# The recurrence's score products of a stick-breaking / HGRN2 / MoE layer, in blocks of 32 tokens instead of 64

## What is computed

```python
b = jnp.cumsum(fb, axis=2)
diff = b[:, :, :, None, :] - b[:, :, None, :, :]
decay = jnp.where(causal, jnp.exp(jnp.where(causal, diff, 0.0)), 0.0)
scores = jnp.einsum('bhtc,bhsc,bhtsc->bhts', qb, kb, decay)
o = jnp.einsum('bhts,bhsv->bhtv', scores, vb) + jnp.einsum('bhtc,bhcv->bhtv', qb * jnp.exp(b), s)
s_new = jnp.exp(b_last[:, :, 0, :])[..., None] * s + jnp.einsum('bhsc,bhsv->bhcv', kb * jnp.exp(b_last - b), vb)
```

## Time and profile before

| | |
|---|---|
| median of 3 runs | 2429.89 us (2425.22 to 2437.62) |
| the profiled execution: its time, its span | 2428.82 us, 2426.9 us |
| TensorE busy | 2284.9 us, 94% of the span |
| VectorE, ScalarE, GpSimd busy | 1405.8, 963.1, 1496.5 us |
| mean granted clock of TensorE | 0.987 of full |

### The profile page before, as it was taken

How to read it: one execution, slowest core, us unless ns; L and a number is a source line. 1 busy time by engine, 2 the same in 40 slices (tenths; PEclk the granted TensorE clock), 3 DMA queues, 4 the chain that set the end, 5 groups by cost and what they waited for, 6 DMA issues and landing times. The chain is left out here.

```text
span 2426.9 us, 40519 instructions
## 1 busy us (share of the span) xinstructions
PE 2284.9 (94%) x15460; PEld 2011.2 (83%) x15460; DVE 1405.8 (58%) x2749; ACT 963.1 (40%) x1582; POOL 1496.5 (62%) x1525
## 2 busy tenths in 40 slices
PE   4999999999999999999998999999999999999882
PEld 4889899898898998989987776578898888888882
DVE  7365665755756647557567697534455555555344
ACT  3452734526436346263364232122323333333334
POOL 6355674675646646657467256577667777776533
PEclk9999999999999999999998999999999999999996
DMA  5201112011011111111112641599999999999995
GB/s 181 77 28 45 41 45 60 29 44 50 29 45 49 46 50 37 36 50 37 47 38 78 194 133 47 154 281 300 310 348 350 354 352 350 351 352 360 363 353 181
DMA packets 210602, 380.72 MB, mean 157 GB/s; under 512 B 25810, under 2 KB 132558, under 8 KB 209898
## 3 DMA queue, kind: packets, MB, share of 16 engines
q1 hardware_dynamic: 180218, 302.25, 34.8%
q0 software_dynamic: 30192, 75.89, 13.1%
HBM read 310.71 MB, written 76.41 MB: 160 GB/s over the span
## 5 line engine op out<-in xcount | busy, mean ns | idle before, releaser
L128 PE MATMUL ps<-xTh,w_mix_low 128*128 128x368 f32 (+1 forms) x1728 | 594.1, 344 | 7.0 <-POOL w_mix_low L122 5.7
L130 PE MATMUL ps<-xTh,w_mix_high 128*128 128x368 f32 (+3 forms) x1808 | 598.9, 331 | 0.4 <-issue 0.4
L129 PE MATMUL ps<-xTl,w_mix_high 128*128 128x368 f32 (+3 forms) x1808 | 597.1, 330 | 1.5 <-issue 1.5
L2298 POOL DMA_INDIRECT xg_early<-h_d,tabq_early x304 | 313.2, 1030 | 153.8 <-issue 80.8
L129 PEld LDWEIGHTS ps<-xTl,w_mix_high 128*128 128x128 f32 (+1 forms) x1808 | 340.1, 188 | 15.8 <-issue 9.5
L128 PEld LDWEIGHTS ps<-xTh,w_mix_low 128*128 128x128 f32 x1728 | 329.3, 191 | 20.5 <-issue 15.4
L130 PEld LDWEIGHTS ps<-xTh,w_mix_high 128*128 128x128 f32 (+1 forms) x1808 | 339.4, 188 | 5.6 <-issue 1.8
L2310 POOL DMA_INDIRECT ys_d<-yo,tab_early x114 | 216.6, 1900 | 112.6 <-issue 50.6
L122 POOL TENSOR_TENSOR w_mix_low<-w_mix_raw,w_mix_high 128x1024 fp32r<-128x1024 f32 x72 | 182.7, 2537 | 120.9 <-ACT w_mix_high L117 83.1
L1333 POOL TENSOR_TENSOR x_m<-x_m,kh_m 128x128 f32<-128x128 f32 (+1 forms) x272 | 125.4, 461 | 114.6 <-ACT x_m L866 114.6
L2340 PEld LDWEIGHTS ps<-xgT,wg_early 128*128 128x128 f32 x1376 | 177.6, 190 | 19.3 <-issue 18.6
(11 more groups left out here) (396 smaller groups left out, 4558.8 us busy)
## 6 DMA issues: line engine op xcount, KB each, us to landing
wd_early<-in_w_exp_down SPq DMA_DIRECT2D x43, 1024.0 KB
wg_early<-in_w_exp_gate SPq DMA_DIRECT2D x82, 512.0 KB
wu_early<-in_w_exp_up SPq DMA_DIRECT2D x82, 512.0 KB
w_mix_raw<-in_w_in SPq DMA_DIRECT2D x72, 512.0 KB, 3.8
wg<-in_w_exp_gate SPq DMA_DIRECT2D x42, 512.0 KB
wu<-in_w_exp_up SPq DMA_DIRECT2D x42, 512.0 KB
wd<-in_w_exp_down SPq DMA_DIRECT2D x21, 1024.0 KB
xg_early<-h_d,tabq_early POOLq DMA_INDIRECT x316
```

The costliest lines, as they stand in the source:

```text
L128: pe.matmul(out, ll, rh, start=start, stop=False)
L129: pe.matmul(out, lh, rl, start=False, stop=False)
L130: return pe.matmul(out, lh, rh, start=False, stop=stop)
L2298: pool.indirect_dma_start(out=xg[:, b, g, :], out_offset=None, in_=h2_d[:, :].rearrange("t (q n) -> (t q) n", q=4), in_offset=bass.Indirec ...
```

## The change

The block becomes 32 tokens, so there are six planes (the diagonal and the levels 1 to 16), and each has up to four products of 32 by 32, which go to four groups of 32 partitions. The level of 32 leaves the masked planes and becomes, like the level of 64, a product between the two halves without a mask (one for each 64 tokens). VectorE masks the six planes (192 columns), copies the level of 32 (two copies of 32x32) and of 64 (one of 64x64) from PSUM into aT, sums the planes of all 128 partitions in one reduce into a compact tile `diagonal`, waits for it, and copies its four blocks into their place in aT. All of aT is cleared once, since more blocks of it stay zero. One mask level less is built at the entry, and the masks are cut out in four copies instead of two. The second meaning of the name LATE is renamed BEHIND, so that the routing reads the constant 65536 again and not 6; no instruction is added or removed by that.

```diff
@@ -56,8 +56,9 @@
 SLOTS = NE * CAP + OVB * P
 LEVELS = [1, 2, 4, 8, 16, 32, 64]
 NL = len(LEVELS)
-BLOCK = 64
+BLOCK, HALF = 32, 64
 PLANES = 1 + sum(2 * hw <= BLOCK for hw in LEVELS)
+ACROSS, HALVES = PLANES * BLOCK, (PLANES + 1) * BLOCK
 CHUNKS = [(0, 368), (368, 368), (736, 352)]
 (C_SQ, C_SK, C_SV, C_HQ, C_HF, C_HI, C_HG, C_GS, C_GH) = range(0, 9 * D, D)
 
...
@@ -368,24 +369,25 @@
+        diagonal = sb("diagonal_m", [P, 2, BLOCK])
-            CONSTANTS = 3 + 3 * (PLANES - 1) + 2 + 2
+            CONSTANTS = 3 + 3 * (PLANES - 1) + 2 + P // BLOCK
...
@@ -676,10 +678,13 @@
                         for i in range(PLANES - 1):
                             for b in range(0, m, BLOCK):
                                 xs = x[:, slot, i, xo + b:xo + b + BLOCK]
-                                mm = pe.matmul(ps[b:b + BLOCK, bank, (i + 1) * BLOCK:(i + 2) * BLOCK], xs, xs, start=True, stop=True)
+                                pe.matmul(ps[b:b + BLOCK, bank, (i + 1) * BLOCK:(i + 2) * BLOCK], xs, xs, start=True, stop=True)
+                        for b in range(0, m, HALF):
+                            mm = pe.matmul(ps[b:b + BLOCK, bank, ACROSS:ACROSS + BLOCK], x[:, slot, NL - 2, xo + b:xo + b + BLOCK],
+                                           x[:, slot, NL - 2, xo + b + BLOCK:xo + b + HALF], start=True, stop=True)
                         if m == P:
-                            mm = pe.matmul(ps[0:BLOCK, bank, PLANES * BLOCK:(PLANES + 1) * BLOCK], x[:, slot, NL - 1, xo:xo + BLOCK],
-                                           x[:, slot, NL - 1, xo + BLOCK:xo + P], start=True, stop=True)
+                            mm = pe.matmul(ps[0:HALF, bank, HALVES:HALVES + HALF], x[:, slot, NL - 1, xo:xo + HALF],
+                                           x[:, slot, NL - 1, xo + HALF:xo + P], start=True, stop=True)
                         mm.then_inc(p_done, 1)
                         if j:
                             pe.wait_ge(ke_copied, j)
...
@@ -1135,14 +1140,17 @@
                             dve.wait_ge(a_done, j - 1)
                             dve.wait_ge(y_done, j - 1)
                         planes = ps[:m, PB[j % 2], 0:PLANES * BLOCK].rearrange("p (l t) -> p l t", l=PLANES)
-                        mm = dve.tensor_tensor(pm[:m, j % 2, :, :], planes, masks[:m, :, :], ALU.mult)
+                        dve.tensor_tensor(pm[:m, j % 2, :, :], planes, masks[:m, :, :], ALU.mult)
+                        for b in range(0, m, HALF):
+                            mm = dve.tensor_copy(aT[b:b + BLOCK, j % 2, b + BLOCK:b + HALF], ps[b:b + BLOCK, PB[j % 2], ACROSS:ACROSS + BLOCK])
                         if m == P:
-                            mm = dve.tensor_copy(aT[0:BLOCK, j % 2, BLOCK:P], ps[0:BLOCK, PB[j % 2], PLANES * BLOCK:(PLANES + 1) * BLOCK])
+                            mm = dve.tensor_copy(aT[0:HALF, j % 2, HALF:P], ps[0:HALF, PB[j % 2], HALVES:HALVES + HALF])
                         mm.then_inc(masked, 1)
                         dve.wait_ge(masked, j + 1)
+                        dve.tensor_reduce(diagonal[:m, j % 2, :], pm[:m, j % 2, :, :].rearrange("p l t -> p t l"), AX.X, ALU.add).then_inc(summed, 1)
+                        dve.wait_ge(summed, j + 1)
                         for b in range(0, m, BLOCK):
-                            mm = dve.tensor_reduce(aT[b:b + BLOCK, j % 2, b:b + BLOCK],
-                                                   pm[b:b + BLOCK, j % 2, :, :].rearrange("p l t -> p t l"), AX.X, ALU.add)
+                            mm = dve.tensor_copy(aT[b:b + BLOCK, j % 2, b:b + BLOCK], diagonal[b:b + BLOCK, j % 2, :])
                         mm.then_inc(a_done, 1)
 
                     def state(cn):
...
@@ -1219,7 +1227,7 @@
                 ch = Chain(dve, entry_s)
                 dve.memset(tri[:, :, :], 1.0).then_inc(memo, 1)
                 dve.memset(whole[:, :, :], 1.0).then_inc(memo, 1)
-                dve.memset(aT[BLOCK:P, :, 0:BLOCK], 0.0)
+                dve.memset(aT[:, :, :], 0.0)
                 dve.memset(small[:, 0:1], RMS_EPS).then_inc(memo, 1)
                 for t in range(NT):
                     statistics(t)
...
@@ -1256,7 +1264,7 @@
                     attention(h)
                     hgrn(h)
                 last_merge()
-                for k in range(EARLY, LATE):
+                for k in range(EARLY, BEHIND):
                     dve.wait_ge(wo_high, k + 1)
                     split_low(dve, wol[:, k, :], staged[k], woh[:, k, :]).then_inc(wo_rest, 1)
                 dve.wait_ge(row_high, 2)
```

More of the change, by code:

```diff
@@ L244, in __exit__ @@
         self.stack.close()
-FIRST, LATE = 5, 6
+FIRST, BEHIND = 5, 6
 COLUMNS = {"q": C_SQ, "k": C_SK, "v": C_SV, "hq": C_HQ, "hf": C_HF, "hi": C_HI, "hg": C_HG, "gs": C_GS, "gh": C_GH}
@@ L375, in mixer @@
                        "z_done abs_done e_done l_done z_copied sp_done hi_done lo_done c_done arg_done w_done o_done "
-                       "osb_copied pa pd diff_done exp_done eb_done qe_exp qe_done x_done p_done masked a_done ke_done ke_copied "
+                       "osb_copied pa pd diff_done exp_done eb_done qe_exp qe_done x_done p_done masked summed a_done ke_done ke_copied "
                        "y_done oT_copied su_done s_done sg_done silu_done g_done squares root_ready u_raw merged wo_in wo_high wo_low last_s par_in xr0 xr1 xr2 xr3 var_ready rstd_ready entry_s shift_ready normed scaled xn_ready turned x_high x_low xs0 xs1 xs2 xs3 "
@@ L380, in mixer @@
                 z_done, abs_done, e_done, l_done, z_copied, sp_done, hi_done, lo_done, c_done, arg_done, w_done, o_done,
-                osb_copied, pa, pd, diff_done, exp_done, eb_done, qe_exp, qe_done, x_done, p_done, masked, a_done, ke_done, ke_copied,
+                osb_copied, pa, pd, diff_done, exp_done, eb_done, qe_exp, qe_done, x_done, p_done, masked, summed, a_done, ke_done, ke_copied,
                 y_done, oT_copied, su_done, s_done, sg_done, silu_done, g_done, squares, root_ready, u_raw, merged, wo_in, wo_high, wo_low, last_s,
@@ L1407, in _ @@
                     hgrn(h)
-    return staged[LATE:]
+    return staged[BEHIND:]
 SHARED_SEMAPHORES = "kept yo0 yo1 yo2 yo3 xi0 xi1 stored0 stored1 y_left y_right x_clear tab_s early_in"
@@ L1512, in _ @@
             m_load(3)
-            sp.wait_ge(wo_low, HEADS - LATE)
+            sp.wait_ge(wo_low, HEADS - BEHIND)
             for dst, n in ((wg, "w_sh_gate"), (wu, "w_sh_up"), (wd, "w_sh_down")):
@@ L1553, in first_tile @@
                 for k in range(FIRST, HEADS):
-                    if k >= LATE:
-                        pe.wait_ge(wo_low, k - LATE + 1)
+                    if k >= BEHIND:
+                        pe.wait_ge(wo_low, k - BEHIND + 1)
                     for b in range(2):
@@ L1910, in tables @@
                     dve.tensor_copy(tabw[:, some, j], ps[:, RB, n * NE:(n + 1) * NE][:, some]).then_inc(tab_s, 1)
-            for k in range(LATE, HEADS):
-                split_low(dve, wol[:, k, :], late[k - LATE], woh[:, k, :]).then_inc(wo_low, 1)
+            for k in range(BEHIND, HEADS):
+                split_low(dve, wol[:, k, :], late[k - BEHIND], woh[:, k, :]).then_inc(wo_low, 1)
             dve.wait_ge(first_high, 1)
```

## The result

The changed kernel is slower, by half a percent. Its median is 2443.63 us (11 runs) against 2432.5 us of the kernel before beside it, ratio 1.005, 95% interval 1.0032 to 1.0067. I had forecast 2412.5 us with a range of 2402 to 2434, and slower had 13%, for a reason that did not come true.

What follows compares the result with a forecast made beforehand. TensorE's issue was taken to bound seven heads, the chain between engines the eighth. Savings of 13.3 us (seven heads) and 4 us (last head), 17.3 in all, from the 2429.89 us median gave 2412.5 us, range 2402 to 2434.

Steps and rivals of the forecast that it cites:

- TensorE's products: TensorE's products of one full chunk in the recurrence, first product to transpose: 0.83 us against 1.08, 0.25 less.
- that rival: Each TensorE record has a floor price (29 ns) however many column groups, making the kernel slower, 2464 us; chance 13%.
- The change of width from 32 to 64: TensorE going from 32-wide to 64-wide products in a full chunk: between nothing and 0.10 us, taken as 0.10.
- What of it arrives: TensorE's saving in heads 0 to 6: chunks 0 and 1 nothing, later ones all, 1.9 us a head, 13.3 in seven.
- the wait for the low weights: TensorE's wait for POOL's weights' low part between chunks 1 and 2: 0.83 us before, 1.3 after, in seven heads.
- the prediction's steps: TensorE's times read from the old trace: 0.17 us for L674, 0.70 for L679's 24 records, 0.10 back to full width.
- The four copies: VectorE's 32x32 copies within SBUF into aT: 0.06 to 0.18 us each, taken as 0.12, 0.48 in all per chunk.
- In heads 0 to 6 all this is covered and worth nothing: VectorE's saving of 0.97 us per chunk lies hidden behind TensorE in the first seven heads, so changes no time there.
- The last head: Eighth head's recurrence, bound by the chain between engines: 4 us less, bounds 1 and 6.
- The unit: VectorE's work on one full chunk's scores, from mask to next instruction: 1.78 us against 2.75, 0.97 less.
- the four units of my sum: VectorE's four score units before the fourth part's differences in the last head: 0.97 us saved each, 3.9 in all.
- the rest: Time from the output projection's first product, behind the barrier, to the end; taken as the same in both kernels.

Runs made afterwards that it cites:

- the direct sums: Changed kernel, but four 32x192 reduces write each block's sum straight into aT, replacing one reduce, its wait and four SBUF copies; 2425.78 us, ratio to before 0.9958.

## Why the prediction was wrong

**TensorE's products: right.** 0.86 us against 0.83, ten steps in 0.33 against 0.32, and four groups at no price per record: 40 records in 0.33 us are 8 ns each. Two side figures of that rival don't follow from its own sum, which gives 2451 us at 25 ns a record, not 2453, and has the kernel slower from some 17 ns on, not 15; nothing else rests on them. The change of width from 32 to 64, which no row of before showed, costs: without it the chunk takes 0.17 us less, though this saving has the shorter steps of the level of 64 in it.

**What of it arrives: too much.** I let chunks 2 to 7 and the chunk of 64 arrive, 1.9 us a head. With the copies out of the way it is 158.9 - 158.0 = 0.9 us. Chunks 0 and 1 are held by POOL as I said (the wait for the low weights 1.2 us, forecast 1.3). But chunks 7 and 8 are held as well, by ACT's chain before its copies of the keys. ACT in the kernel before, the chain's first row and the copy at its end:

```profile
240.02 0.48 ACT L787 ACTIVATE kT_m<-ps 128x368 f32<-128x368 f32 x1 [3.73 <-PE ps L130]
...
247.24 0.28 ACT L879 ACTIVATE ke_m<-ps 128x128 f32<-128x128 f32 x1
```

The chain begins behind a product of TensorE just ahead of chunk 7 (240.57), so the gain of chunk 6 still arrives, and what follows does not: from the start of chunk 6 to the last transpose it is 12.99 us before and 12.79 with the direct sums. The 0.98 us of the chunk of 64 were nearly all work (0.17 + 0.70 + 0.10 by the prediction's steps), but ACT's copy of the keys ended only 0.05 us before its transpose in the trace of before, and a shorter chunk just waits for it. What is left is chunks 2 to 6, some 0.2 us each.

**The four copies: the step that failed.** "The four copies in SBUF are in no row; between 0.06 and 0.18 start to start". Alone they take 0.18. Beside POOL they stand, 0.64 in the mean and up to 8.9 us. I looked for the price of the instruction and not for what it needs. The page of the Trainium skill that I cited gave the speed of such a copy; the Trainium skill also has the rule for the ports that it takes (cited above), which I didn't weigh. And the trace of before had the pattern, in a row of my own: the last line of the earlier trace rows is one difference with two sources in SBUF that took 2.29 us, where the thirteen behind it took 0.28 each. It ended 0.16 us behind this one, the last of POOL's products:

```profile
1300.90 0.71 POOL L1335 TENSOR_TENSOR x_m<-x_m,kh_m 128x256 f32<-128x256 f32 x1
```

The same happens the other way round. POOL's second product of a head, 0.5 us elsewhere, and VectorE's fifteen differences with two sources in SBUF beside it:

```profile
168.54 0.67 POOL L1333 TENSOR_TENSOR x_m<-x_m,kh_m 128x128 f32<-128x128 f32 x1 [2.63 <-ACT x_m L866]
169.17 3.65 POOL L1333 TENSOR_TENSOR x_m<-x_m,hq_m 128x128 f32<-128x128 f32 x1
```
```profile
169.19 2.90 DVE L1125 TENSOR_TENSOR x_m<-bT_m 128x128 f32<-128x128 f32 x14
172.02 0.41 DVE L1128 TENSOR_TENSOR x_m<-bT_m 128x256 f32<-128x256 f32 x1
```

VectorE's fifteen end at 172.43 and POOL's instruction at 172.82: the engines exclude each other, and in both places over a whole queue.

**"In heads 0 to 6 all this is covered and worth nothing": wrong.** VectorE's 9 us in chunk 0 are covered where they stand, but they move POOL's split, and TensorE pays 0.5 us for it at chunk 3. In the chunk of 64 both copies meet POOL's two long products and vrow is next in VectorE's queue: 1.4 us more. Measured, the copies cost 159.8 - 158.0 = 1.8 us a head, 12.6 in seven, and 3.1 more through the clock.

**The last head: the wrong sign.** Forecast 4 us less; it takes 4.8 more with the copies in SBUF, and 0.9 less with the sums in PSUM. The unit takes 2.2 us when nothing stands, forecast 1.78: the small copies out of PSUM cost 0.19 and not 0.13 each, and those in SBUF 0.18 and not 0.12. So a unit saves 0.55 us and not 0.97, some 2 us in the four units of my sum; why only 0.9 of them arrive no run shows.

Summed by the profiled executions: entry 2.6, seven heads 9.5 (6.4 of the copies net of the gain, 3.1 of the clock), last head 4.8, the rest 3.6 less, 13.4 in all (rounded), as the spans have it. The entry and the rest differ about as much between executions of kernels that do not differ there; that they nearly cancel is luck.

## What to carry to other kernels

Before an instruction is added to VectorE, look not only for its duration but at what POOL does at that time: a copy, a scaling or an operation with two sources, all in SBUF, can stand for POOL's work, while the same with a source in PSUM does not. A result that is only passed on is then better kept in PSUM. A stall that is covered where it stands can still come out elsewhere: the 8.9 us of chunk 0 became 0.5 us of TensorE at chunk 3. A saving on TensorE arrives only in those chunks that nothing else ends; where another engine ends just ahead of TensorE, as ACT did by 0.05 us in the chunk of 64, there is nothing to gain, though the trace shows no wait.

## What I had not expected of the hardware

A copy of 32x32 stood 8.9 us through the rest of one POOL instruction and fifteen more, and POOL's product 3.6 us through fifteen of VectorE's; in isolation the two took turns instruction by instruction. A step of four column groups of 32, one record in each group, took 33 ns. A wait of TensorE of 1.7 us was followed by some 6 us at half clock in 2 of 21 cases, a wait of 3.3 us by the same low clock in 6 of 7.
